# The chunk recurrence of a hybrid layer, begun behind the q product and stepped by numbered turns

## The reference, cut to what matters

```python
h = rmsnorm(x, norm1_g) * (1.0 + sc1) + sh1
(aq, ak, av, iq, ik, iw, bq, bf, bi, bg, ...) = split_cols(h @ w_in)
f = lb + (1.0 - lb) * jax.nn.sigmoid(f_pre)       # f_pre = bf
log_f = jnp.log(f); kk = 1.0 - f
# o_t = sum over s <= t of (q_t . exp(b_t - b_s) k_s) v_s,  b = cumsum(log_f), v = bi
```

## Time and profile before

| | us |
|---|---|
| median of 3 runs | 2207.91 |
| lowest, highest | 2207.51, 2208.7 |
| the profiled execution, its own time | 2203.48 |
| its span in the trace | 2201.6 |
| TensorE busy in the span | 1992.5 (91%) |
| VectorE, ScalarE, GpSimd busy | 1111.1, 861.2, 123.2 |
| mean granted TensorE clock, share of full | 0.963 |

### The profile page before, as it was taken

The page is one execution under the profiler, slowest core; times in us unless marked ns, Lnnn a source line. Parts: engine busy times, 40 slices in busy tenths (PEclk is TensorE's granted clock), DMA queues, the critical chain, the costliest instruction groups (busy, mean ns, idle before and its releaser), DMA issues.

```text
span 2201.6 us, 30516 instructions
## 1 busy us (share of the span) xinstructions
PE 1992.5 (91%) x12952; PEld 1619.2 (74%) x12952; DVE 1111.1 (50%) x1418; ACT 861.2 (39%) x1131; POOL 123.2 (6%) x110
## 2 busy tenths in 40 slices
PE   8988899999999766676789999999999999969998
PEld 8988688889997211111148997888998999858997
DVE  6455495567764111011126555655556555675554
ACT  5444345554443100000024445545445444645443
POOL 0023212000210000000000000000000000020000
PEclk9999899999999998988899999999999999989999
DMA  9633344567888999999994655545554655305652
GB/s 375 202 97 98 96 139 148 172 197 248 290 316 324 391 424 423 423 424 423 422 386 162 231 191 159 185 157 169 191 191 137 209 185 183 131 20 173 199 174 76
DMA packets 242015, 503.17 MB, mean 229 GB/s; under 512 B 9681, under 2 KB 158514, under 8 KB 217426
## 3 DMA queue, kind: packets, MB, share of 16 engines
q1 hardware_dynamic: 241200, 500.27, 62.9%
q10 hardware_dynamic: 530, 0.73, 0.1%
q0 software_dynamic: 144, 0.17, 0.1%
HBM read 500.07 MB, written 1.06 MB: 228 GB/s over the span
## 4 chain that ended last, share of the span: by engine, by line
PE 72%; DMA 16%; DVE 6%; ACT 2%; issue 2%; POOL 1%; SPq 1%; DVEq 0%; POOLq 0%; ACTq 0%
PE bank L579 21%; PE bank L580 20%; PE bank L581 20%; DMA m<-in_expert_w_up 7%; DMA m<-in_expert_w_down 7%; PE bank L977 2%; PE bank L988 2%; DVE m L2025 1%; PE bank L732 1%; DMA m<-in_ffn_w_in 1%; PE bank L864 1%; DVE m L2678 0%; DMA m<-in_ada_w 0%; PE bank L636 0%; ACT m L1398 0%
## 5 line engine op out<-in xcount | busy, mean ns | idle before, releaser
L579 PE MATMUL bank<-m,m 128*128 128x256 f32 (+2 forms) x3240 | 1025.4, 316 | 20.0 <-DVE m L2025 6.9
L580 PE MATMUL bank<-m,m 128*128 128x256 f32 (+2 forms) x3240 | 1010.4, 312 | 0.0
L581 PE MATMUL bank<-m,m 128*128 128x256 f32 (+2 forms) x3240 | 1009.4, 312 | 0.0
L2025 DVE TENSOR_TENSOR m<-m,m 128x1024 fp32r<-128x1024 f32 x508 | 623.1, 1233 | 404.1 <-ACT m L1398 403.4
L1398 ACT ACTIVATE m<-m 128x1024 fp32r<-128x1024 f32 x508 | 531.4, 1056 | 383.3 <-PE bank L581 357.1
L579 PEld LDWEIGHTS bank<-m,m 128*128 128x128 f32 x3240 | 615.2, 190 | 66.4 <-issue 15.2
L580 PEld LDWEIGHTS bank<-m,m 128*128 128x128 f32 x3240 | 614.8, 190 | 37.6 <-issue 2.4
L581 PEld LDWEIGHTS bank<-m,m 128*128 128x128 f32 x3240 | 614.6, 190 | 36.9
L977 PE MATMUL bank<-m,m 128*32 128x512 f32 x1024 | 188.0, 683 | 67.3 <-DMA m<-in_expert_w_up 46.9
L977 PEld LDWEIGHTS bank<-m,m 128*32 128x32 f32 x1024 | 41.7, 122 | 205.0 <-DMA m<-in_expert_w_up 88.3
L988 PE MATMUL bank<-m,m 128*32 128x512 f32 x512 | 97.0, 721 | 34.1 <-DMA m<-in_expert_w_down 27.9
(11 more groups left out here) (353 smaller groups left out, 1349.7 us busy)
## 6 DMA issues: line engine op xcount, KB each, us to landing
m<-in_ffn_w_in SPq DMA_DIRECT2D x88, 1024.0 KB, 5.1
m<-in_expert_w_gate SPq DMA_DIRECT2D x64, 1024.0 KB, 24.4
m<-in_expert_w_up SPq DMA_DIRECT2D x64, 1024.0 KB, 23.6
m<-in_w_in SPq DMA_DIRECT2D x63, 1024.0 KB, 5.1
m<-in_expert_w_down SPq DMA_DIRECT2D x60, 1024.0 KB, 25.4
m<-in_ffn_w_out SPq DMA_DIRECT2D x44, 1024.0 KB, 4.9
m<-in_ada_w SPq DMA_DIRECT2D x24, 1024.0 KB, 5.5
m<-in_a_w_in SPq DMA_DIRECT2D x16, 1024.0 KB, 5.2
```

The costliest lines, as they stand in the source:

```text
L579: e.matmul(o, s[0], m[0], start=first, stop=False, skip_group_check=skip)
L580: e.matmul(o, s[0], m[1], start=False, stop=False, skip_group_check=skip)
L581: return e.matmul(o, s[1], m[0], start=False, stop=last, skip_group_check=skip)
L2025: inc(e.tensor_tensor(rv(fit(q.L, q.view.shape)), q.view, fit(q.H, q.view.shape), ALU.subtract), "l", skey(q, "L"))
```

## The change

- `hgrn()` is spawned ahead of `bi` in place of behind `iq`, with rate 1 in place of 2. On ACT and DVE, which wait there for the constants, the wait moves too.
- The yields are gone. Each engine has one loop over numbered steps, one for each piece. Half `hf` has n = step - 16 hf. ACT, DVE and GpSimd do level li at n = 2 li + 1, TensorE at n = 2 li + 2: both tiles in one step. The diagonal is TensorE's n = 1 and DVE's n = 2, the output TensorE's n = 17 and ACT's n = 18, the last copy of level 7 ACT's n = 16. DVE merges level li - 1 behind its part of level li. A level is two pieces.
- ACT takes the exponential of S first and of P second, in place of P first. Both logarithms are taken in its first step, in place of one in each half.
- TensorE's last step is its 34th; there are 38 pieces from `bi` to the end of `av`.

The core of the diff (of the functions that stay in substance the same, a line or two):

```diff
@@ tensor
+                for step in range(34):
+                    for hf in range(2):
+                        n = step - 16 * hf
+                        if n == 1:
+                            diagonal(hf)
+                        elif n in range(2, 17, 2):
+                            level(hf, n // 2 - 1)
+                        elif n == 17:
+                            output(hf)
+                    yield
...
+            w.wait_ge("consts")
+            ticks.spawn(hgrn())
             gemm1("bi", hT, h_ready)
             gemm2("iq", hT, h_ready)
-            w.wait_ge("consts")
-            ticks.spawn(hgrn(), 2)
@@ scalar, level
+                    inc(e.activation(Ev[:, 0], Sv[:, :, 0, :], ACT.Exp), "hgrn", ("hgte2", hf, li))
...
+                    inc(e.activation(Ev[:, 1], Pv[:, :, 1, :], ACT.Exp), "hgrn", ("hgte", hf, li))
@@ vector
+                for step in range(32):
+                    for hf in range(2):
+                        n = step - 16 * hf
+                        if n == 2:
+                            diagonal(hf)
+                        elif n in range(1, 16, 2):
+                            level(hf, n // 2)
+                            if n > 1:
+                                masked(hf, n // 2 - 1)
                     yield
@@ gpsimd
+                for step in range(32):
+                    for hf in range(2):
+                        n = step - 16 * hf
+                        if n == 0:
+                            begin(hf)
+                        elif n in range(1, 16, 2):
+                            level(hf, n // 2)
                     yield
```

More of the change, by code:

```diff
@@ L721, in hgrn, with level, output @@
                         full(ins, "hgd", hf, tile)
[L722 to L734, removed]
+                def level(hf, li):
+                    w.wait_ge("hgtQ", hf, li)
+                    w.wait_ge("hgtK", hf, li)
+                    for tile in range(2 if li < 7 else 1):
+                        b = take("s", "hgl", hf, li, tile)
+                        for g in range(4):
+                            c = slice(256 * g + 128 * tile, 256 * g + 128 * tile + 128)
+                            c2 = c if li < 7 else slice(256 * g + 128, 256 * g + 256)
+                            ins = e.matmul(b[:, 128 * g:128 * g + 128], K_[:, c], Q_[:, c2], start=True, stop=True)
+                        full(ins, "hgl", hf, li, tile)
+                def output(hf):
                     w.wait_ge("taken", ("hgl", hf, 6, 1))
@@ L1475, in hgrn @@
[L1475 to L1499, removed]
@@ L1502, in hgrn @@
                                   "hgl", hf, 7, 0)
[L1503 to L1508, removed]
+                        elif n == 18:
+                            for t in range(2):
+                                b = got("hgo", hf, t)
+                                o = 1024 * t + 512 * hf
+                                taken(e.activation(ob[:, o:o + 512], b[:, :], ACT.Copy), "hgo", hf, t, also=[("ob", hf, t)])
+                    yield
             def attention():
@@ L2127, in hgrn, with diagonal @@
             def hgrn():
[L2128 to L2131, removed]
+                S_, Q_, K_, E_ = hg
+                def diagonal(hf):
                     for t in range(2):
@@ L2169, in hgrn, with level @@
-                    yield
+                def level(hf, li):
+                    o = slice(1024 * hf, 1024 * hf + 1024)
+                    h = 1 << li
+                    n = 1024 // (2 * h)
+                    Pv, Qv, qv = [z.rearrange("p (n two h) -> p n two h", two=2, h=h) for z in (bf[:, o], Q_, bq[:, o])]
+                    Ev = E_.rearrange("p (two n h) -> p two n h", two=2, h=h)
+                    w.wait_ge("hgte", hf, li)
+                    if li:
+                        w.wait_ge("full", ("hgl", hf, li - 1, 1))
+                        w.wait_ge("hgtQ", hf, li - 1)
+                    else:
+                        w.wait_ge("hgQ", hf)
+                    inc(e.tensor_tensor(Qv[:, :, 1, :], qv[:, :, 1, :], Ev[:, 1], ALU.mult), "hgrn", ("hgtQ", hf, li))
+                    if li < 7:
+                        w.wait_ge("hgtS", hf, li)
+                        if li:
+                            w.wait_ge("hgtP", hf, li - 1)
+                        inc(e.tensor_tensor(Pv[:, :, 1, :], Pv[:, :, 1, :], Pv[:, :, 0, h - 1:h].to_broadcast([128, n, h]),
+                                            ALU.add), "hgrn", ("hgtP", hf, li))
@@ L2928, in hgrn, with begin @@
             def hgrn():
-                for hf in range(2):
-                    o = slice(1024 * hf, 1024 * hf + 1024)
-                    k_, P_, (S_, Q_, K_, E_) = bk[:, o], bf[:, o], hg
+                S_, Q_, K_, E_ = hg
+                def begin(hf):
                     if hf:
```

128 lines of the change are left out of this document (57 added, 71 removed).

## The result

The changed kernel takes 2182.87 us, median of 4 runs (2182.03 to 2183.36), against 2207.71 us of 4 runs of before (2205.07 to 2208.70): a ratio of 0.9889, with a 95% interval of 0.9872 to 0.9906. That is 24.8 us less; forecast were 26.4 us less and 2181.5 us. The profiled execution took 2183.36 us, its span 2181.6.

A forecast was written before the change was run, and what follows sets the result against it. TensorE was the bound, held up by the recurrence's turns of other engines. Work 145.0 + waits 5.6 + clock 1.6 = 152.2 us against 178.8; less 0.2 for the tables, 2207.9 - 26.4 = 2181.5 us, range 2176 to 2190 (75%).

The forecast's parts named there:

- The waits: TensorE waiting for K and Q: nine turns with one copy 0.42 us each, two in `bi` 0.91, 5.6 us in all.
- the turn of 3.27 us: From a piece's end T through copy, exponential, K and Q: TensorE starts at T + 3.27 us, wanted at T + 2.85.
- Q slowed by K: At each level DVE's Q meets GpSimd's K and takes 1.31 us, about twice 0.69, ready at T + 3.21.
- DVE's slack: DVE, the tightest engine, is free at T + 8.4 us, next Q wanted at T + 9.6: 1.2 us of slack.
- period of 7.7 us: Time between two levels: two pieces, a pair of tiles and the wait; used to reckon when the next Q is wanted.
- The first K: GpSimd's first K of the recurrence, under `bi`, is wanted at about 84.2 us.
- The unrecorded instruction: GpSimd instruction ahead of its first K, absent from the trace: between 0 and 37.7 us, once; taken as 0.
- The third rival: GpSimd's unrecorded instruction holds up the first K and the whole recurrence: up to 37.7 us, 2219 us; chance 6%.
- The table loads: ACT's two function table loads before the first level, taken as hidden by a 2.85 us piece; otherwise some 2.6 us late.
- The clock behind `iw`: Half clock behind the narrow `iw` piece stays as before: some 3.3 us at half, cost 1.6 us; no other drop.
- 0.08 us of restart: First matmul behind a recurrence turn takes 0.36 us in place of 0.28: 18 turns, 1.4 us.
- Behind `av`: Attention's wait for its tables stays: 9.2 us from `av`'s end to its first matmul against 9.0, about 6.2 idle.

The follow-up runs named there:

- x5: Changed kernel with one empty step ahead of the numbered ones on every engine, so levels fall at even pieces, where no product ends: 2176.67 us, ratio 0.9865.
- x2: Changed kernel, but TensorE takes a level in the same turn as the other engines make it, without the lag of one piece: 2243.32 us, ratio 1.0161.
- x1: Changed kernel with ACT's exponential of P ahead of that of S again: 2184.66 us, ratio 0.9896.
- x6: Changed kernel with the `iw` product's eight columns read sixteen times over, so each matmul has 128 columns: 2179.10 us, ratio 0.9874.
- x4: Changed kernel with its numbered steps spawned behind `iq`, as before, in place of ahead of `bi`: 2198.84 us, ratio 0.9959.
- x3: Kernel before with its unchanged generator, at the old rate of 2, spawned ahead of `bi` in place of behind `iq`: 2211.18 us, ratio 1.0020.
- x7: Changed kernel with SP's two loads of the attention's tables issued ahead of the weight load of `cq`'s fourth piece: 2173.95 us, ratio 0.9859.

## Why the prediction was right, and where its terms were off

The profiled executions can be set beside the sum step by step.

- **The waits: right.** Forecast were 9 of 0.42 and 2 of 0.91 us, 5.6 in all. The trace shows 4.3: nine of 0.27 to 0.34, and 0.88 and 0.76 in `bi`. The view counts idle time from the end of the last matmul, which is 0.28 long and ends 0.16 us after the next could have started (the pitch is 0.12). Counted as in the sum, from T + 2.85, a wait is 0.43 to 0.50, and the two in `bi` are 1.05 and 0.92, 6.1 us in all. x5 and x2 show the cause, the copy ahead and the turn of 3.27 us.
- **Q slowed by K: right.** 1.36 us at nearly every level. By the Trainium skill, "GPSIMD Engine Reference", section 8, the two contend where VectorE reads two SBUF inputs; the trace agrees, Q taking 1.36 us and ending 0.54 us behind K, where the same instruction takes 0.69 in x1 with GpSimd idle. K takes 1.29 us in both.
- **DVE's slack: right where a product ends.** Forecast 1.2 us, measured 1.43 ahead of Q. The forecast's period of 7.7 us was added up too low: its own terms make 7.8, and two levels are 124.87 - 116.84 = 8.0 us apart. At turn 5, in `bi` and without a copy, there was no slack: Q started at 101.05 us with no idle time before it, took 0.68 us since GpSimd was idle, and ended 0.08 us before TensorE's pair at 101.81. That this stayed free of a wait is partly luck; in x1 the same turn has one of 0.85 us.
- **The first K: right.** The unrecorded instruction cost nothing that shows. GpSimd's copies took 1.04 and 1.03 us, the first K started at 83.86 us (forecast 84.2) and waited for ACT. The third rival falls.
- **The table loads: hidden, as taken.** Each took 1.28 us, and the next instruction started 0.01 us behind it:

```profile
77.55 1.28 ACT L1481 ACT_TABLE_LOAD   x1
78.84 2.01 ACT L1481 ACTIVATE m<-m 128x1024 f32<-128x1024 f32 x2
```

By "ScalarE: Activation LUTs" of the Trainium skill, "What ACT_TABLE_LOAD costs", it would have been 2.66 us with the drain; the trace shows half of it here, and the measurement decides.

- **The clock behind `iw`: the term that was mis-sized.** I took over before's 3.3 us at half clock, at 1.6 us. In the changed kernel it is 6.8 us (windows of 1 us: 0.85 at 132, 0.50 from 133 to 138, 0.73 at 139), at 3.4 us. The step that failed is "that piece is as narrow as before": the piece was, the stretch around it was not as short. x6 shows that the piece causes it. What sets its length isn't settled: 3.4 us before, 6.8 after, 3.4 in x5, some 10 in x4, 14 in x3, in and behind the same 48 matmuls. In x3 a wait of 2.9 us stands right ahead of it and the narrow matmuls themselves run at half clock; before, x4 and x5 have no such wait, and x4 a long stretch all the same. (The page's line of the granted clock dips in slice 36 too, which the prediction passes over; that lies behind what the change touches.)
- **A term that was left out.** Behind a wait, the pair of tiles costs 120.07 - 118.26 = 1.81 us; without a wait 160.33 - 158.63 = 1.70, the value I used. That is 11 times 0.11, 1.2 us. The 0.08 us of restart that the sum had is that of the piece behind the pair.
- **Behind `av`: right.** From its end to the attention's first matmul 241.12 - 231.83 = 9.3 us (forecast 9.2), with 6.25 idle (forecast 6.2). Both points came later than forecast, at 231.8 and 241.1 us in place of 228 and 237.5. SP issued the tables right behind the weight load of its turn:

```profile
231.83 0.28 PE L579 MATMUL bank<-m,m 128*128 128x256 f32 x1
...
235.43 0.37 SPq L3092 DMA_DIRECT2D m<-in_w_in  x1
235.84 0.58 SPq L3151 DMA_DIRECT2D m<-in_rel_bias  x1
236.46 0.42 SPq L3152 DMA_DIRECT2D m<-in_buckets  x1
...
241.12 1.44 PE L765 MATMUL bank<-m,m 32*8 32x384 f32 x2 [6.25 <-DMA m<-in_buckets]
```

- **The sum.** From `bi`'s first matmul (75.79 us) to `av`'s end it took 156.0 us; forecast were 152.2. Of the 3.8 us more, 1.8 are the clock around `iw`, 1.2 the pairs behind waits, and 0.5 the waits (6.1 in place of 5.6); 0.3 is not accounted for. The attention so started 22.8 us earlier and not 26.4.
- **The total.** The medians say 24.8 us, the two profiled executions 2203.48 - 2183.36 = 20.1. The second differs from the 22.8 by 2.7 us of the later stages, which the table of experiments shows to vary by up to 4.2 us between two kernels. It differs from the medians since the profiled execution of before was itself 4.2 us below its median, and the changed one 0.5 above its own. The forecast was made against the median, and so part of its closeness (1.4 us) is chance: on the trace its mechanism promised 3.6 us too much, and the profiled execution was 6.4 us slower than forecast (2177).

## What to carry to other kernels

Where TensorE waits for a chain over several engines, give it the result one piece of its own work later, and count first whether there are pieces enough: here the lag started late gave 8 us, the early start alone -4, both 25. Put such turns where the helpers have nothing ahead of them (x5), and load the small things ahead of a queue's next large one (x7). Narrow matmuls can lose the clock for themselves and for what comes behind them; x6 made them wide at no cost.

## What the runs showed of the hardware

- A matmul with 8 columns and one with 128 follow each other at the same 0.11 us, and at half clock the 8 columns take 0.21 (144.80 to 145.01 us in x3). What sets the 0.11 isn't the columns. With 256 columns it is 0.12 us and with 512 columns 0.23 (231.83 to 231.95 and 231.13 to 231.36 us after).
- In and behind the same narrow piece the stretch at half clock was 3.4 us (before, x5), 6.8 (after), 10 (x4) and 14 us long (x3). In the changed kernel the clock was still 1.00 for the first 3 us of the narrow matmuls (128 to 131 us) and fell while they ran.
- A wait doesn't always cost the clock. In the kernel before, windows of 1 us show half clock behind five of the nine waits of line 732; behind the one that ends at 165.16 us, 3.11 us long, the clock stayed at 1.00, and behind one of 3.22 us, which ends at 204.64 us, it was 0.50.
- VectorE's multiplication with two inputs in SBUF (128x512, f32) takes 0.69 us with GpSimd idle and 1.36 beside GpSimd's multiplication of the same size, which started 0.47 us earlier and takes 1.29 us either way (x1 against after). It ends 0.54 us behind GpSimd's.
- The first 16 matmuls behind a wait of 0.3 us take 0.11 us longer than without it, at a granted clock of 1.00 (window 118 to 121 us after).
